# Layer 0's input product with six of eight chunks split, and modulation weights in half-step pieces of 512 KB

## What is computed

```python
sh_a, sc_a, ga, sh_f, sc_f, gf = split(silu(c) @ w_ada[l] + b_ada[l], 6)   # the same from c_ctx for context rows
z = (x * (1 + sc_a) + sh_a) @ w_in[l]                 # 1024 -> 1440 columns
q_a, kv_a, k_rope, gq, gk, gv = split(z)
q  = rms_norm(q_a) @ w_q_b[l];  kv = rms_norm(kv_a) @ w_kv_b[l]
gq, gk = rms_norm per head; 2-D rotary on q_rope, k_rope, gq, gk
x = layer_norm(ALPHA * x + ga * (attention(...) @ w_o[l]), ln1_g[l], ln1_b[l])
x = layer_norm(ALPHA * x + gf * moe(x * (1 + sc_f) + sh_f), ln2_g[l], ln2_b[l])   # top-2 of 32 experts
```

## Time and profile before

| | us |
|---|---|
| median of three runs (3457.48 to 3462.58) | 3459.23 |
| the profiled execution's own time | 3460.31 |
| its span, first to last instruction | 3458.4 |
| busy: PE / DVE / ACT / POOL | 3150.2 / 2617.7 / 1777.9 / 1394.6 |
| layer 0 projections in the trace | about 4.9 to 354 |
| layer 1 projections | about 1762 to 2064 |
| final combine | from 3397.4 |

### The profile page before, as it was taken

The page is one execution under the profiler, slowest core; times in us unless marked ns, Lnnn a source line. Parts: engine busy times, 40 slices in busy tenths (PEclk is TensorE's granted clock), DMA queues, the critical chain, the costliest instruction groups (busy, mean ns, idle before and its releaser), DMA issues. The chain is left out here.

```text
span 3458.4 us, 44535 instructions
## 1 busy us (share of the span) xinstructions
PE 3150.2 (91%) x14820; PEld 2254.5 (65%) x14820; DVE 2617.7 (76%) x2451; ACT 1777.9 (51%) x2048; POOL 1394.6 (40%) x1043
## 2 busy tenths in 40 slices
PE   6999699998895999999969979999989699999995
PEld 3776455544584888888847755554448488888882
DVE  3444566777687999999968857777868799999995
ACT  2333233343312888888844442334341388888883
POOL 2221011111212777777722210111111388888882
PEclk8999799999997999999989998999999799999997
DMA  7766723121545988879855556312134589799865
GB/s 293 261 243 209 190 76 73 56 69 52 196 147 199 367 310 353 312 292 385 338 189 171 162 157 157 77 43 71 41 113 181 218 301 380 297 364 353 327 257 215
DMA packets 288169, 734.59 MB, mean 212 GB/s; under 512 B 62440, under 2 KB 169360, under 8 KB 236712
## 3 DMA queue, kind: packets, MB, share of 16 engines
q0 software_dynamic: 109328, 502.86, 39.0%
q1 hardware_dynamic: 164344, 182.16, 17.2%
q10 hardware_dynamic: 14368, 47.99, 3.9%
HBM read 723.65 MB, written 124.37 MB: 245 GB/s over the span
## 5 line engine op out<-in xcount | busy, mean ns | idle before, releaser
L2414 DVE TENSOR_TENSOR ex_wl<-ex_back,ex_wh 128x2048 fp32r<-128x2048 f32 x288 | 652.2, 2291 | 94.5 <-ACT ex_wh L2328 94.5
L1403 ACT ACTIVATE at_pt<-at_st 128x1024 f32<-128x1024 f32 x328 | 335.3, 1024 | 545.0 <-PE at_st L1317 543.1
L2328 ACT ACTIVATE ex_wh<-ex_back 128x2048 fp32r<-128x2048 f32 x288 | 551.2, 1920 | 30.6 <-PE ex_vp L2259 17.2
L1462 DVE TENSOR_REDUCE at_nm<-at_sc 128x1 f32<-128x1280 f32 x246 | 365.5, 1486 | 198.5 <-PE at_sc L1279 195.3
L1476 DVE TENSOR_TENSOR at_acc<-at_acc,at_pt 128x1024 f32<-128x1024 f32 x256 | 322.7, 1260 | 99.7 <-ACT at_pt L1403 97.7
L2414 DVE TENSOR_TENSOR ex_wl<-ex_front,ex_wh 128x2048 fp32r<-128x2048 f32 x144 | 324.2, 2291 | 11.5 <-ACT ex_wh L2328 11.5
L2157 POOL DMA_INDIRECT ex_back<-in_w_down,piece_of x144 | 300.8, 2089 | 46.0 <-issue 43.4
L2328 ACT ACTIVATE ex_wh<-ex_front 128x2048 fp32r<-128x2048 f32 x144 | 275.2, 1922 | 84.5 <-SPq L2197 60.3
L1344 PE MATMUL at_op<-at_pt,at_va 128*64 128x512 f32 x1280 | 306.9, 609 | 0.2
L1317 PE MATMUL at_st<-at_q,at_km 96*128 96x512 f32 (+3 forms) x1008 | 265.6, 404 | 4.5 <-DVE at_nm L1462 4.0
L1317 PEld LDWEIGHTS at_st<-at_q,at_km 96*128 96x128 f32 (+1 forms) x1008 | 179.4, 192 | 98.0 <-issue 56.0
(11 more groups left out here) (320 smaller groups left out, 6692.3 us busy)
## 6 DMA issues: line engine op xcount, KB each, us to landing
ad_w<-in_w_ada POOLq DMA_DIRECT2D x48, 1024.0 KB, 9.9
heads<-T SPq DMA_DIRECT2D x80, 512.0 KB, 7.6
at_q<-heads SPq DMA_DIRECT2D x80, 256.0 KB, 4.2
at_km<-heads SPq DMA_DIRECT2D x16, 640.0 KB, 10.0
mr_ot<-o_s SPq DMA_DIRECT2D x18, 512.0 KB, 5.3
h_s<-mr_h ACTq DMA_DIRECT2D x18, 512.0 KB, 2.7
cy<-y_s POOLq DMA_DIRECT2D x9, 1024.0 KB, 7.4
at_rinv<-inv_s POOLq DMA_DIRECT2D x68, 128.0 KB, 2.9
```

The lines of the kernel that those rows point to most:

```text
L1403: nc.scalar.activation(pt[:, j % PT, :, 0:nq], st[:, j % 2, :, 0:nq], ACT.Exp).then_inc(exp_done, 1)
L1462: nc.vector.tensor_reduce(nm[:, v % 3, s:s + 1], bank[:, 0:kb * P], AX.X, ALU.max, negate=True).then_inc(max_done, 1)
L2328: nc.scalar.activation(wh[:, q], early.raw(u, p), ACT.Copy).then_inc(hi_done, 1)
L2414: nc.vector.tensor_tensor(wl[:, q], early.raw(u, p), wh[:, q].bitcast(F32), ALU.subtract).then_inc(lo_done, 1)
```

## The change

The constants: `NS_FIRST` goes from 4 to 6, and the modulation weights' buffers from four of 1 MB (two chunks) to four of 512 KB (one chunk). `ad_load(step, half)` and `part_ad(step, half)` now treat half a step, four chunks. In tile t PE executes `part_ad(t + 1, 0)` behind `part_qa(t - 1)` and `part_ad(t + 1, 1)` behind the split chunks of banks 0 and 1. POOL's order for a tile becomes `ad_load(t + 1, 1)`, `norm(t - 1)`, `norm_low(t)`, `ad_load(t + 2, 0)`; in the tail `ad_load(11, 1)` stands ahead of `norm(9)`, and PE's second half of step 11 stands last. SP's weight loads of layer 0 wait for the third landing in buffer 0, and load the six split chunks ahead of the two plain ones. The stores of `ada` move behind those of the last tile, and are awaited by SP in attention.

In layer 1's head the first expert row moves from POOL's queue to SP's, and the bias row `ln2_b` from ACT's to SP's behind it; ACT's last two `w_hi` copies move behind the modulation of tile 0; two of DVE's `w_lo` subtractions move back; PE gets 7 filling matmuls (`keep_busy`, 512 columns of float32) once the first row is there. In attention three of ACT's five first loads move behind its first copy of ones. In the final combine the bias row moves from ACT's queue to SP's, behind the second tile's load, and PE gets 4 filling matmuls at the start.

```diff
-AD_N, AD_Q, AD_K, AD_BUF = 1024, 256, 2, 4
+AD_N, AD_Q, AD_BUF = 1024, 256, 4
 AD_STEPS = DEPTH * 6 * D // AD_N
-NS_FIRST, NS_LATER = 4, 6
+NS_FIRST, NS_LATER = 6, 6
 NS_EARLY = 4
...
             if first_layer:
-                sp.wait_ge(ad_full[0], 32)
+                sp.wait_ge(ad_full[0], 48)
             else:
+                sp.dma_start(cy[:, 0, :], S["y_s"].rearrange("(t p k) n -> t p k n", p=P, k=TOPK)[0][:, 0, :]).then_inc(zero_y_loaded, 16)
+                sp.wait_ge(zero_y_loaded, 16)
+                sp.dma_start(late[:, 1, :], A["ln2_b"][layer - 1].partition_broadcast(P)).then_inc(rows_loaded, 16)
                 sp.wait_ge(old_x, 16)
...
                     put(t - 1, g, q_stored[g])
-            if first_layer:
-                sp.wait_ge(ad_out, AD_STEPS + 1)
-                ada = S["ada"].rearrange("s (i j n) -> s i j n", j=4, n=AD_Q)
-                for j in range(4):
-                    sp.dma_start(ada[:, :, j, :], ad_row[32 * j:32 * j + 2, :, :]).then_inc(ad_stored, 16)
             t = NT - 1
...
             if first_layer:
-                sp.wait_ge(ad_stored, 65)
+                sp.wait_ge(ad_out, AD_STEPS + 1)
+                ada = S["ada"].rearrange("s (i j n) -> s i j n", j=4, n=AD_Q)
+                for j in range(4):
+                    sp.dma_start(ada[:, :, j, :], ad_row[32 * j:32 * j + 2, :, :]).then_inc(R["ada_stored"], 16)
             sp.wait_ge(v_stored, 16 * t + 1)
...
-            if not first_layer:
-                pool.dma_start(cy[:, 0, :], S["y_s"].rearrange("(t p k) n -> t p k n", p=P, k=TOPK)[0][:, 0, :]).then_inc(y_loaded, 16)
+            def ad_load(step, half):
+                for b in range(AD_BUF):
+                    k = half * AD_BUF + b
+                    if step or half:
+                        pool.wait_ge(ad_used, KC * step + k - AD_BUF + 2)
+                    pool.dma_start(ad_w[:, b], ad_piece(step, k)).then_inc(ad_full[b], 16)
+
             if first_layer:
-                for q in range(AD_BUF):
-                    pool.dma_start(ad_w[:, q], ad_piece(0, q)).then_inc(ad_full[q], 16)
                 nc.gpsimd.memset(ad_silu[:, :, :], 0.0).then_inc(ad_clear, 1)
+                ad_load(0, 0)
                 nc.gpsimd.memset(ad_row[:, :, :], 0.0).then_inc(row_clear, 1)
...
                     pool.dma_start(ad_row[32 * j:32 * j + 2, :, :], bias[j].partition_broadcast(2)).then_inc(ad_bias, 16)
-                for q in range(AD_BUF):
-                    pool.wait_ge(ad_used, q + 2)
-                    pool.dma_start(ad_w[:, q], ad_piece(1, q)).then_inc(ad_full[q], 16)
+                ad_load(0, 1)
+                for half in range(2):
+                    ad_load(1, half)
             if first_layer:
...
-            def ad_load(step):
-                for q in range(AD_BUF):
-                    pool.wait_ge(ad_used, AD_BUF * (step - 1) + q + 2)
-                    pool.dma_start(ad_w[:, q], ad_piece(step, q)).then_inc(ad_full[q], 16)
-
             if first_layer:
                 pool.wait_ge(w_loaded, 33)
-                ad_load(2)
+                ad_load(2, 0)
                 norm_low(0)
-                norm(0)
-                ad_load(3)
-                norm_low(1)
-                for t in range(2, NT):
-                    ad_load(t + 2)
+                for t in range(1, NT):
+                    ad_load(t + 1, 1)
                     norm(t - 1)
                     norm_low(t)
+                    ad_load(t + 2, 0)
+                ad_load(AD_STEPS - 1, 1)
                 norm(NT - 1)
...
             nc.scalar.activation(modt[:, CT:NT], mod[:, 1:2].to_broadcast([P, LT, 2, KC]), ACT.Copy).then_inc(modt_ready, 1)
-            split_w((0,) if first_layer else range(HERE, NS))
+            if first_layer:
+                split_w((0,))
             act.wait_ge(modt_done, 2)
             modulate(0)
-            if first_layer:
-                split_w(range(1, NS))
+            split_w(range(1 if first_layer else HERE, NS))
             if first_layer:
...
             else:
-                split_w(range(HERE))
+                split_w(range(HERE - 2))
                 dve.wait_ge(R["rows_loaded"], R["early_rows"])
...
                 spread_of(0)
+                split_w((HERE - 2,))
                 dve.wait_ge(rows_loaded, 16)
...
             modulate(0)
-            split_w(range(1 if first_layer else HERE, NS))
+            split_w(range(1 if first_layer else HERE - 1, NS))
             if not first_layer:
...
                     gated(combine)
-                if step is not None:
-                    ad_take(step)
                 turn_queries(t)
...
                     finish(combine)
+                if step is not None and order == range(4):
+                    ad_take(step)
                 take_heads(t, (2, 3), order)
+                if step is not None and order != range(4):
+                    ad_take(step)
...
-            def part_ad(step):
-                for q in range(AD_BUF):
-                    if q == 0:
+            def part_ad(step, half):
+                for b in range(AD_BUF):
+                    k = half * AD_BUF + b
+                    if k == 0:
                         pe.wait_ge(ad_out, step + 1)
-                    pe.wait_ge(ad_full[q], 16 * (step + 1))
-                    for k in range(q * AD_K, (q + 1) * AD_K):
-                        for j in range(4):
-                            ins = nc.tensor.matmul(adp[32 * j:32 * j + 32, 0:AD_Q], ad_silu[:, k, :],
-                                                   ad_w[:, q, k % AD_K, j * AD_Q:(j + 1) * AD_Q],
-                                                   start=(k == 0), stop=(k == KC - 1))
+                    pe.wait_ge(ad_full[b], 32 * step + 16 * (half + 1))
+                    for j in range(4):
+                        ins = nc.tensor.matmul(adp[32 * j:32 * j + 32, 0:AD_Q], ad_silu[:, k, :],
+                                               ad_w[:, b, j * AD_Q:(j + 1) * AD_Q],
+                                               start=(k == 0), stop=(k == KC - 1))
                     ins.then_inc(ad_used, 1)
...
                 pe.wait_ge(silu_done, 2)
-                part_ad(0)
-                part_ad(1)
+                for step in range(2):
+                    for half in range(2):
+                        part_ad(step, half)
                 pe.wait_ge(ad_out, 3)
...
                 pe.wait_ge(mod_taken, 2)
+            else:
+                pe.wait_ge(zero_y_loaded, 16)
+                keep_busy(nc, C, zp[:, 2, :], 7)
...
                 if first_layer:
-                    if not first:
-                        part_ad(t + 1)
+                    part_ad(t + 1, 0)
                 elif first:
...
                         part_z(t, n, k)
-                if first_layer and first:
-                    part_ad(2)
+                if first_layer:
+                    part_ad(t + 1, 1)
                 if first:
...
             if first_layer:
-                part_ad(AD_STEPS - 1)
+                part_ad(AD_STEPS - 1, 0)
             part_up(NT - 1)
             part_heads(NT - 1, tail=True, order=LAST)
+            if first_layer:
+                part_ad(AD_STEPS - 1, 1)
...
             sp.wait_ge(R["tail_stored"], 48 * (layer + 1))
+            sp.wait_ge(R["ada_stored"], 64)
             load_q(sp, 1, 0, 0)
...
             load_k(act, 0, 0, 1)
-            load_k(act, 0, 1, 1)
-            load_q(act, 0, 1, 1)
-            load_q(act, 1, 0, 1)
             ones = C["ones"][:, 0:1]
             for s in range(2):
+                if s == 1:
+                    load_k(act, 0, 1, 1)
+                    load_q(act, 0, 1, 1)
+                    load_q(act, 1, 0, 1)
                 nc.scalar.activation(km[QK:QK + 1, s, 0].rearrange("p h n -> p (h n)"),
...
                     sp.wait_ge(y_loaded[0], 16)
+                if t == 1:
+                    sp.dma_start(bias[:, :], A["ln2_b"][layer].partition_broadcast(P)).then_inc(norm_loaded, 16)
             for t in range(nt):
...
         def _(act):
-            act.dma_start(bias[:, :], A["ln2_b"][layer].partition_broadcast(P)).then_inc(norm_loaded, 16)
-
             for t in range(nt):
...
         def _(pe):
+            keep_busy(nc, C, ps[1], 4)
             for t in range(nt):
...
```

More of the change, by code:

```diff
@@ L245, in projections @@
         if first_layer:
-            ad_w = sb("ad_w", [P, AD_BUF, AD_K, AD_N])
+            ad_w = sb("ad_w", [P, AD_BUF, AD_N])
             ad_row = sb("ad_row", [P, AD_STEPS, AD_Q])
@@ L296, in up_cols, with ad_piece @@
             return slice(k * NQ, (k + 1) * NQ) if k < 3 else slice(3 * NQ + (k - 3) * NKV, 3 * NQ + (k - 2) * NKV)
-        def ad_piece(step, q):
+        def ad_piece(step, k):
             at = step * AD_N
             w = A["w_ada"][at // (6 * D)].rearrange("(p a) n -> p a n", a=KC)
-            return w[:, q * AD_K:(q + 1) * AD_K, at % (6 * D):at % (6 * D) + AD_N]
```

(10 more changed lines are left out.)

4 lines of the change are left out of this document (2 added, 2 removed).

## The result

The changed kernel takes 3482.56 us (median of five, 3477.62 to 3490.91), the one before 3459.23 beside it: 1.0069, 95% interval 1.0054 to 1.0085, or +23.9 us by the ratio (+19 to +29; the medians lie 23.3 apart). The forecast was 3467, with a range up to 3478. The profiled execution took 3477.62 us, the fastest of the five; its span is 3475.7.

What follows compares the result with a forecast made beforehand. PE alone was taken to set the pace in layer 0's loop. Terms -9.3 + 16.8 + 2.4 + 9.0 - 2.3 - 1.5 - 4.8 - 3.3, plus 0.6, gave +7.6: 3467 us, range 3453 to 3478.

Steps and rivals of the forecast that it cites:

- The loop's wait: Layer 0's loop: PE waits some 2.1 us per tile for modulation pieces, 16.8 us in tiles 2 to 9.
- Rivals 1 and 2: Loop's pieces land in time, 3450 us, chance 0.13; or small piece's fixed part is 1.8 us, 3458 us, chance 0.25.
- The product: Layer 0's input product: two more split chunks save 0.93 us per tile, 9.3 us in ten tiles.
- halved step: Layer 0's modulation step on PE: each half taken as 3.66 / 2 = 1.83 us, with no extra cost for halving.
- The head: Start of layer 0: tile 0's product starts later because its plain chunks load last, +2.4 us.
- my bound of +6: Layer 0's head: modulation loads lose their share of the engines to w_in, so shift and scale come late, +6 us.
- The tail: End of layer 0: late part_up(9) and norm(9), and ada's stores moved last, +9.0 us (+5 to +12).
- Attention: Start of attention: earlier stores and reordered loads bring first scores sooner, -2.3 us in layer 0, -1.5 in layer 1.
- Layer 1's head and the combine: Layer 1's head: PE starts before the last copies, -4.8 us; combine: moved bias load and filling matmuls, -3.3 us.
- Rival 3: Load latency costs more at head (+6), beside each tile's pieces (+9) and tail (+3): 3482 us, chance 0.14.

Runs made afterwards that it cites:

- e1: Changed kernel with GpSimd issuing the first half of step t + 2 ahead of norm_low(t) instead of behind it; 3462.1 us, ratio 1.0010.
- f3: Changed kernel with SP's layer 0 weight loads released by the fourth landing in buffer 0 instead of the third; 3484.4 us, ratio 1.0074.
- e5: Changed kernel with pieces issued ahead of norm_low, norm(9) ahead of the last half step's loads, plain chunks first behind a later gate; 3460.5 us, ratio 1.0004.
- f1: Kernel before with only the change's edits outside layer 0's product (layer 1's head, ACT's attention load order, combine); 3457.7 us, ratio 1.0000.
- h1: Second run of the kernel before with only the change's edits outside layer 0's product; 3455.8 us, ratio 0.9985.
- g1: Changed kernel with early issue, head's order, and one more modulation half step in tile 1, step 11's second half loaded a tile earlier; 3459.4 us, ratio 1.0000.

## Why the prediction was wrong

- **The loop's wait** was right, and it is the step that decides: 18.0 measured by e1 against 17.4 (17.2 in the waits themselves), period 31.1 against 30.6, the landing times within 0.3 us. So the measured row (a 1 MB piece in 5.4 us) was the right guide. By the Trainium skill's rule (DMA: Bandwidth & Descriptors, section on the anatomy of one SWDGE DMA) the estimate of the wait was 1.0 per tile; 2.3 were seen in the tile above. Rivals 1 and 2 fall.
- **The product** was right: 0.92 us per tile against 0.93. But the **halved step** was put at nothing (each half at 3.66 / 2 = 1.83), and it costs 0.30 per tile, 3 us in ten. This is why the loop shows 6.0 and not 9.3 from before to e1.
- **The head** was +5.6 and not +2.4, near my bound of +6, and by the mechanism that I gave for the bound: the weights lose their share of the engines to w_in, and the shift and scale come last. f3 shows the contest with w_in (5.3 us sooner behind a later gate); that it is the 2 MB in flight instead of 4 is argued, not tried. The late plain chunks, on which I based +2.4, are hidden behind that.
- **The tail** was the right size, 8.0 against 9.0, but with part of the mechanism missing, so the match is partly luck. I counted part_up and norm(9) as late, and they were (r_tok 5.7 us later than before against tile 8's heads). But with both in place again (e5) the tail stays at 35.0: behind them stood the stores of the heads, slowed by the last 2 MB. The prediction gave that slowing no price.
- **Attention** gives 0.4 instead of 2.3 in layer 0 and 0.1 instead of 1.5 in layer 1: the scores wait for at_km as before.
- **Layer 1's head and the combine**: the places and signs were right (about -4.1 and -2.4 to -3.3 in their stages against -4.8 and -3.3), but of layer 1's 4.1 only some 3 last to the end of its stage in ten traces, and next to nothing in the four where the clock falls at its last heads.
- Together: halved step and product +3.1, head +3.2, loop +0.6, tail -1.0, attention +3.4, layer 1 +1.5, combine 0 to +0.9 above the forecast's +7.6 make 18 to 19. So the steps that failed are the halved step put at nothing, the head taken at +2.4 for +5.6, and the gains of attention and layer 1's head. Measured is 23.9 (19 to 29). The 5 us between the two are left open; they are no larger than the interval. Rival 3 had the time, 3482, and the head, but not the mechanism of the rest: stores beside the pieces were to cost 9 us in the loop, and there the landings were on schedule.

No version here clearly beats the kernel before. The nearest is before with the edits of f1 and h1; among kernels with six split chunks in layer 0, e5 and g1 tie with it.

## What to carry to other kernels

A buffer cut in half halves the time that hides its refill, so first look up what stands ahead of the refill on the issuing engine: here 20 of 24 us came back by issuing four DMAs ahead of one small operation. Where two things arrive within a few us of each other, undo them together as well as singly before calling either free, and at a stage's end count the bytes on the DMA engines before the order on the compute engines. A piece of work cut in two costs more than the whole, here 0.30 us per cut, and it adds up over the tiles. And book the gains as carefully as the losses: mine were about half of the error that the terms explain.

## What the runs showed of the hardware

- TensorE's granted clock was 1.00 through a loop in which it never waited, and fell to 0.5 (of its two levels, 2.4 to 1.2 GHz) for about 3.5 us behind gaps that add up to some 2.3 us in a tile. Of seven traces with eight such tiles each it did so once in four and never in three; in the changed kernel's trace it cost 1.7 us.
- Pieces of 512 KB issued 0.54 us apart could be used 1.3 to 1.4 us apart in the loop. In the head, where each issue waits for its buffer and w_in's loads run beside them, it was 2.9 to 3.1.
- The same kernel spreads by up to 21 us (e1: 3452.0 to 3473.0 in twelve runs), with a mean granted clock of 0.966 in the fastest and 0.961 in the slowest; but a run of 3460.4 had 0.959, so the clock alone doesn't order them. The kernel before spreads by 10 to 20.
- Layer 1's first row of y, moved from POOL's queue to SP's, was issued 3.2 us after ACT's (1791.02, 1794.23), where POOL had issued it 0.4 after. This wasn't tried by itself.
